# One scaled input for two norms, norm weights and shifts as columns at evictions, and a strict mask added by a matrix product, in the attention chain of a two-block network

## The reference

```python
def modulate(h, shift, scale):
    return h * (1.0 + scale[:, None, :]) + shift[:, None, :]
# keys and values: h = modulate(rmsnorm(x, kv_norm_g), shift, scale) @ kv_w, and k = rmsnorm(k per head, k_norm_g)
# queries:         h = modulate(rmsnorm(x, norm_mix_g[1]), sh1, sc1) @ w_q,  and q = rmsnorm(q per head, q_norm_g) * 64**-0.5
z = q . k                                        # 16 heads of 64, queries in blocks of 128
strict = jnp.arange(end)[None, :] < (t0 + jnp.arange(SB_BLOCK))[:, None]
log1m = jnp.where(strict, -jax.nn.softplus(z), 0.0)
between = lax.cumsum(log1m, axis=3, reverse=True) - log1m
a = jnp.where(strict, jnp.exp(jax.nn.log_sigmoid(z) + between), 0.0)
out = a @ v, then @ w_out
```

## Time and profile before

| what | value |
|---|---|
| median of 3 runs | 3055.77 us (3055.34 to 3058.81) |
| the profiled execution | 3056.06 us, span 3054.3 us |
| busy in the span | PE 67%, DVE 58%, ACT 28%, POOL 33% |
| mean granted clock of TensorE | 0.826 |
| POOL's gathers (L743) | 512 of u rows, 512 of v rows |
| DMA over the span | 862.77 MB, mean 282 GB/s |

### The profile page before, as it was taken

The page is one execution under the profiler, slowest core; times in us unless marked ns, Lnnn a source line. Parts: engine busy times, 40 slices in busy tenths (PEclk is TensorE's granted clock), DMA queues, the critical chain, the costliest instruction groups (busy, mean ns, idle before and its releaser), DMA issues.

```text
span 3054.3 us, 33874 instructions
## 1 busy us (share of the span) xinstructions
PE 2043.3 (67%) x11630; PEld 1413.7 (46%) x11630; DVE 1778.2 (58%) x3285; ACT 840.6 (28%) x1268; POOL 1011.0 (33%) x1063
## 2 busy tenths in 40 slices
PE   7888710355426746257520357998899989988998
PEld 3636400011112212122100014996799879877997
DVE  2365689913694356970769403666566566655664
ACT  3434200000021101221000002445554454555444
POOL 1000067777565575654777772001000000000000
PEclk9999955677757978569755677999899999999999
DMA  7575699999999999989999996554155545542553
GB/s 277 190 261 195 224 376 420 406 392 416 420 393 358 418 407 416 385 313 419 400 419 420 410 419 236 185 184 149 48 174 184 176 144 185 172 134 80 181 184 126
DMA packets 238775, 862.77 MB, mean 282 GB/s; under 512 B 27958, under 2 KB 28428, under 8 KB 238404
## 3 DMA queue, kind: packets, MB, share of 16 engines
q0 software_dynamic: 147456, 536.94, 43.9%
q1 hardware_dynamic: 87840, 318.81, 30.6%
q10 hardware_dynamic: 3364, 5.61, 0.6%
HBM read 860.18 MB, written 1.05 MB: 282 GB/s over the span
## 4 chain that ended last, share of the span: by engine, by line
PE 37%; DVE 16%; DMA 12%; issue 11%; POOL 10%; ACT 2%; DVEq 1%; ACTq 0%; POOLq 0%
PE ps L1417 17%; POOL sb_arena L743 10%; DVE sb_arena L2447 9%; DMA sb_arena<-in_peer_v,sb_arena 8%; PE ps L1428 7%; DMA sb_arena<-in_peer_u,sb_arena 4%; PE ps L831 4%; PE ps L1178 3%; PE ps L993 1%; DVE sb_w_lo L638 1%; PE ps L1211 1%; PE ps L1335 1%; PE ps L868 1%; ACT sb_arena L2000 0%; PE ps L1026 0%
## 5 line engine op out<-in xcount | busy, mean ns | idle before, releaser
L638 DVE TENSOR_TENSOR sb_w_lo<-sb_w,sb_w_hi 128x1024 fp32r<-128x1024 f32 (+2 forms) x393 | 470.6, 1212 | 330.9 <-ACT sb_w_hi L624 327.7
L2447 DVE CUSTOM_DVE_ANT_0 sb_arena<-sb_arena,ps 128x1024 f32<-128x1024 f32 x512 | 607.1, 1219 | 60.7 <-DMA sb_arena<-in_peer_u,sb_arena 50.4
L743 POOL DMA_INDIRECT sb_arena<-in_peer_u,sb_arena x512 | 486.2, 950 | 352.9 <-issue 118.8
L743 POOL DMA_INDIRECT sb_arena<-in_peer_v,sb_arena x512 | 494.8, 966 | 250.9 <-issue 140.7
L1178 PE MATMUL ps<-sb_arena 128*32 128x512 f32 x2048 | 349.9, 816 | 268.6 <-DMA sb_arena<-in_peer_v,sb_arena 265.9
L624 ACT ACTIVATE sb_w_hi<-sb_w 128x1024 fp32r<-128x1024 f32 (+2 forms) x398 | 407.5, 1040 | 291.7 <-DMA sb_w<-in_ffn 197.9
L1417 PE MATMUL ps<-sb_xT_hi,sb_w_hi 128*128 128x256 f32 x1408 | 400.2, 284 | 2.8 <-DVE sb_w_lo L638 2.8
L1417 PE MATMUL ps<-sb_xT_hi,sb_w_lo 128*128 128x256 f32 x1408 | 400.1, 284 | 0.0
L1417 PE MATMUL ps<-sb_xT_lo,sb_w_hi 128*128 128x256 f32 x1408 | 400.0, 284 | 0.0
L1178 PEld LDWEIGHTS ps<-sb_arena 128*32 128x32 f32 x2048 | 75.2, 131 | 524.6 <-issue 521.7
L638 POOL TENSOR_TENSOR sb_w_lo<-sb_w,sb_w_hi 128x1024 fp32r<-128x1024 f32 x5 | 11.7, 2350 | 918.9 <-ACT sb_w_hi L624 596.7
(11 more groups left out here) (426 smaller groups left out, 3001.7 us busy)
## 6 DMA issues: line engine op xcount, KB each, us to landing
sb_w<-in_ffn SPq DMA_DIRECT2D x264, 512.0 KB, 3.5
sb_w<-in_ada_w SPq DMA_DIRECT2D x112, 512.0 KB, 6.2
sb_w<-in_peer_w_q SPq DMA_DIRECT2D x48, 512.0 KB, 8.0
sb_w<-in_kv_w SPq DMA_DIRECT2D x32, 512.0 KB, 8.4
sb_w<-in_fox_w_in SPq DMA_DIRECT2D x24, 512.0 KB, 3.3
sb_w<-in_ma_w_vo SPq DMA_DIRECT2D x16, 512.0 KB, 3.5
sb_arena<-in_peer_u,sb_arena POOLq DMA_INDIRECT x512, 6.8
sb_arena<-in_peer_v,sb_arena POOLq DMA_INDIRECT x512, 6.7
```

The costliest lines, as they stand in the source:

```text
L638: e.tensor_tensor(lo, w, hi.bitcast(F32), ALU.subtract).then_inc(lo_ready, 1)
L743: pool.indirect_dma_start(ROW[:, r % ROWS, :], None, d[("peer_v" if kind else "peer_u") + str(layer)], bass.IndirectOffsetOnAxis(ap=(LISTE ...
L2447: v.tensor_tensor_reduce(out=x, in0=x, in1=PS[:, 0:2, :].rearrange("p a b -> p (a b)"), scale=1.0, scalar=0.0, op0=ALU.mult, op1=ALU.add, ...
```

## The change

- VectorE scales `x` by the root alone, once (`row_factor` and one `ts`), and TensorE transposes that once. ScalarE's evictions of the transposes, now eight of 128x128 for keys and eight for queries instead of two of 128x512 each, multiply with a column (norm weight times 1 + scale) and add a column (shift), which lie in `gain_cols`. The queries' transposed input has a buffer of its own (`w_xqT`) and a semaphore `queries_taken`.
- The weights of the head norms are multiplied in at the evictions of the transposed heads.
- `before` is gone. TensorE begins the diagonal block of each score bank with a product of `upto` and a new matrix `never` (zero but for -1e30 on the diagonal), which adds -1e30 wherever the key is not strictly earlier; the scores are accumulated on it. Both masks and the minimum with 0 go, and exp signals `att_ready` itself.
- Six small loads are added to ScalarE's in table 0 (20 instead of 14), 32 transposes of 1x128 on TensorE in its tick 4, and ScalarE's copies and 16 products of 128x1 that make the columns.
- Of the copies on all partitions only one (`norm_ffn_g1`) is left, loaded ahead of the stage and multiplied with 1 + scale once.
- The transpose of the list of experts is written in tick 8 of the u tables instead of tick 20.

```diff
+            pool.affine_select(out=never[:, :], in_=never[:, :], compare_op=ALU.not_equal, fill=-MASKED,
+                               base=0, pattern=[[-1, P]], channel_multiplier=1)
...
# PE
+                        for n, x in enumerate((mod(1), KVMOD[:, D:2 * D], mod(0), KVMOD[:, 0:D])):
+                            for k_ in range(KD):
+                                tr(PS[:, 3, 128 + KD * n + k_:129 + KD * n + k_], x[0:1, k_ * P:(k_ + 1) * P], ident[0:1, 0:1])
...
-                        if k == 20:
+                        if k == 8:
...
+                        for odd in range(2):
+                            mm(PS[:, 3 + odd, 0:(t + 1) * 2 * P].rearrange("p (a b s) -> p a b s", a=2, s=P)[:, :, t, :],
+                               upto[:, :], never[:, :].unsqueeze(1).to_broadcast([P, 2, P]), start=True, stop=False,
+                               skip_group_check=True)
...
-                    pe.wait_ge(SEM["normed"], 3 * t + 2)
-                    turned(H[:, t, :])
+                    pe.wait_ge(SEM["queries_taken"], t + 1)
...
# ACT
+                    def moved_in(dst, which, b, turn_):
+
+                        for c in range(4):
+                            scale, shift = moved(4 * b + c)[which]
+                            ins = f(dst[:, 4 * b + c, :], PS[:, 3 + turn_ % 2, c * P:(c + 1) * P], ACT.Identity,
+                                    scale=scale, bias=shift)
+                        return ins
...
-                    taken(w_kT[:, :, t * P:(t + 1) * P])
-                    next_gain(4, 4)
+                    taken(w_kT[:, :, t * P:(t + 1) * P], gain=gain_cols[:, KEY_GAIN:KEY_GAIN + 1])
...
-                        f(x, x, ACT.Exp).then_inc(SEM["exp_out"], 1)
+                        f(x, x, ACT.Exp).then_inc(SEM["att_ready"], 1)
...
# DVE
-                        dve.drain()
-                        masked(w_lost).then_inc(SEM["lost_ready"], 1)
+                        dve.drain().then_inc(SEM["lost_ready"], 1)
...
-                    norm(0, KVMOD[:, 0:D], KVMOD[:, D:2 * D])
+                    row_factor(1)
+                    ts(h, x, rs[:, ROOT:ROOT + 1], None, ALU.mult).then_inc(SEM["normed"], 1)
                     yield "norm for keys"
-                    dve.wait_ge(SEM["tile_turned"], 16 * t + 2)
-                    norm(1, mod(0), mod(1))
...
-                    for n, y in enumerate(both):
-                        tt(y, y, gain_of(2 + n, SD).unsqueeze(1).to_broadcast([P, SH, SD]), ALU.mult
...
-                           ALU.subtract)
-                        dve.drain()
-
-                        ts(y, y, 0.0, None, ALU.min).then_inc(SEM["exponent_in"], 1)
+                           ALU.subtract).then_inc(SEM["exponent_in"], 1)
                         yield "between"
-                        dve.wait_ge(SEM["exp_out"], 4 * t + g + 1)
-                        masked(y).then_inc(SEM["att_ready"], 1)
```

More of the change, by code:

```diff
@@ L86, in build @@
         after = sb("after", [P, P])
-        before = sb("before", [P, P])
+        never = sb("never", [P, P])
         upto = sb("upto", [P, P])
@@ L225, in build @@
         stage("weave", loads=loads * NT, gain=len(gains))
-        for _ in range(NT):
-            gains.extend([("kv_norm_g", D), ("norm_mix_g1", D), ("k_norm_g", SD), ("sb_q_norm_g", SD), ("norm_ffn_g1", D)])
+        gains.append(("norm_ffn_g1", D))
         def embed(i):
@@ L534, in build, with moved @@
         w_head_gains = WHF[:, 4224:4288]
+        WOVEN_GAINS = (("norm_mix_g1", KD), ("kv_norm_g", KD))
+        KEY_GAIN, QUERY_GAIN = 74, 75
+        def moved(n):
+            return [gain_cols[:, x + n:x + n + 1] for x in (84, 100)], [gain_cols[:, x + n:x + n + 1] for x in (76, 92)]
         def by_block(x, t):
@@ L691, in _ @@
             pool.memset(ones[:, :], 1.0)
+            pool.memset(never[:, :], 0.0)
             pool.memset(causal[:, :], 0.0)
@@ L1184, in chain @@
                 def chain(t):
-                    turns, cols, units = 16 * t, 12 * t, st["unit0"] + len(st["loads"]) // NT * t
+                    turns, cols, units = 14 * t, 12 * t, st["unit0"] + len(st["loads"]) // NT * t
                     def turned(src, jobs=2):
@@ L1199, in turned, with column @@
                             turns += 1
-                    def column():
+                    def column(x=w_xT):
                         nonlocal cols, units
@@ L1228, in scores @@
                                              w_kT[rows, g * HG // 2 + pair, b * P:(b + 1) * P],
-                                             w_qT[rows, g * HG // 2 + pair, :], start=True, stop=True)
+                                             w_qT[rows, g * HG // 2 + pair, :], start=b < t, stop=True,
+                                             skip_group_check=True)
                         pe.drain().then_inc(SEM["z_ready"], 1)
@@ L1723, in gather @@
                             row += n
+                        for name in ("k_norm_g", "sb_q_norm_g"):
+                            for c in range(2):
+                                act.dma_start(w_gains[row:row + 1, c * SD:(c + 1) * SD], d[name].unsqueeze(0)
+                                              ).then_inc(gains_loaded, 16)
+                            row += 1
+                        for name, n in WOVEN_GAINS:
+                            act.dma_start(w_gains[row:row + n, :], d[name].rearrange("(k p) -> k p", p=P)
+                                          ).then_inc(gains_loaded, 16)
+                            row += n
                         for row, name in enumerate(("fox_g_qn", "fox_g_kn", "mla_g_qn", "mla_g_kn")):
@@ L1794, in chain @@
                     stats(0)
-                    next_gain(1, 0)
                     yield "norm for keys"
-                    taken(w_xT)
-                    next_gain(2, 1)
+                    for b in range(2):
+                        act.wait_ge(SEM["tile_turned"], turns + b + 1)
+                        moved_in(w_xT, 0, b, turns + b).then_inc(SEM["tile_taken"], 1)
+                    for b in range(2):
+                        ins = moved_in(w_xqT, 1, b, turns + b)
+                    ins.then_inc(SEM["queries_taken"], 1)
+                    turns += 2
                     yield "turn for keys"
```

85 lines of the change are left out of this document (39 added, 46 removed).

## The result

The changed kernel takes 3049.23 us (median of 10 runs, 3044.88 to 3052.07) against 3057.05 us (3051.96 to 3060.36) for the kernel before on the same chip: ratio 0.9975, 95% interval 0.9965 to 0.9984. The gain is 8 us; 31 were predicted, and the time lies above the range. The profiled execution took 3050.52 us, span 3048.8.

A forecast was written before the change was run, and what follows sets the result against it. The gather stage was taken as bound by DMA at 420 GB/s, with VectorE later behind tick 13; 18.9 (VectorE) + 8.4 (change of table) + 3.75 (bytes) = 31 us off 3056.06 gave 3025 us, range 3010 to 3043.

The forecast's parts named there:

- the sum: Forecast gain: 18.9 us of VectorE's work, 8.4 at the change of table, 3.75 of bytes, together 31 us.
- VectorE behind tick 13: After the head sums: products, masks and minima removed from VectorE, 8.9 us in block 0, 10.0 in block 1.
- Rival B: Behind tick 13 irregularly landing rows swallow half of VectorE's 18.9 us: 3034 us; chance 0.18 (3030 to 3045).
- The change of table: Between VectorE's last dot and the GELU: shorter wait, 4.3 us in block 0, 4.1 in block 1, together 8.4.
- Bytes: In the gather stage: five 512 KB weight copies leave, three of them counted at 1.25 us each, 3.75 us.
- (a) the mask products: Ahead of each group's scores: two added TensorE products, 1 us per group, at most 2.1, hidden by 2.5 us slack.
- (b) the wait for `between`: Between a group's first `lost` and its `between`: VectorE may wait some 0.2 us where the mask went.
- (c) the sixteen evictions: Per block, 128x128 evictions replacing four of 128x512: at most 6 us of ScalarE, costing nothing; uncovered, 3 us per block.
- (d) the small loads: Table 0: six more loads on ScalarE's queue, first dot 1.6 to 2.1 us later, hidden; if not, +2 us.
- The word on POOL: Beside one-input VectorE operations gathers wait 0.26 us: eight minima removed save up to 2.1 us, new scalings cost 2 x 0.26.
- Rival A: In the gather stage all 41.7 us of losses and 6.25 us of bytes return: 3008 us; chance 0.12 (below 3015).
- Rivals C and D: C: scores-to-softplus path becomes the bound, 3065 us, chance 0.04; D: chain no shorter, only bytes go, 3052 us, 0.04.

The follow-up runs named there:

- the first experiment: The changed kernel with eight small tensors packed into one, so the gathers' slots start on a multiple of 256 bytes again: 3027.26 us, ratio 0.9900.
- the second: The kernel before with 128 unused bytes ahead of the arena, so the slots start 128 bytes past a multiple of 256: 3080.36 us, ratio 1.0076.

## Why the prediction was wrong

**The step that failed** is the first: "The rest of the stage is DMA-bound, and there only bytes count", at 420 GB/s and 1.25 us for a gather. The plateau was taken as a constant, and the losses and the sum were counted from it. It is not one: the same diff moved the slots 128 bytes, and a gather of 512 KB costs 1.28 us. For the stage's 1024 gathers that is 537 MB x (1/409.5 - 1/420) = 33 us at most, 8.2 for a pair of tables; the first experiment gives 22 and the second 23. Between the changed kernel and the first experiment tables 0 and 1 differ by all of it, 8.4 us, the pairs with the chain by only 4.3 and 5.3: from the head sums to the last dot VectorE takes the same 96 and 103 us in both kernels, whatever a gather costs. No part of the sum, of its bounds or of the rivals held a change of the DMA's own pace, and so the range was too narrow. With the slots on the boundary the time is 3027.3 us against 3025 forecast. The three kernels that differ from the changed one in memory layout alone and have the slots there gain 30 (packed tensors), 34 (all of memory) and 37 us (only the slots moved) over before; the sum's 31 fits them.

The diff line that did it was read, as more columns for weights and shifts. What was not done was to ask which tensor is allocated behind it.

**The prediction's other steps:**

- *VectorE behind tick 13, 18.9 us*: right in its mechanism, and in size as far as the runs tell. From head sums to the last dot it takes 95.8 us in block 0 (842.5 to 938.3), as forecast, and in block 1 1235.05 to 1338.5 = 103.5, 1.5 above. Put back, the work costs 17 us, with an uncertainty of about 7. Rival B (half swallowed, 9.5) is not supported: in neither block does VectorE wait for a row behind tick 13 in the changed kernel. All of its waits in block 1's stretch are these:

```profile
DVE sb_w_hi_whole L2577 <- PE ps L1255: 0.8, 1, 0.8
DVE sb_arena L2478 <- issue: 0.6, 4, 0.2
DVE sb_w_hi_whole L2567 <- issue: 0.4, 1, 0.4
```

- *The change of table, 8.4 us*: right in its mechanism (waits of 0.42 and 2.33 us where 0.5 and 2.4 were said); put back, it costs 12.5 us by the ratio with an uncertainty of about 7, 10 by the table pairs, and 8.7 in the two stretches that it lengthens.
- *Bytes, 3.75 us*: neither shown nor excluded.
- *(a) the mask products*: they took the upper bound in block 1, 2.08 us for the first group, and used the slack up: VectorE takes that group's first operation at 1258.89, 0.03 us after ScalarE's end (1257.80 + 1.06); it was 2.5 before. The cost is still nothing, but the cover is gone in that group.
- *(b) the wait for `between`*: one of 0.8 us, where some 0.2 was said.
- *(c) the sixteen evictions*: 5.7 us of ScalarE in block 0, within the 6 allowed.
- *(d) the small loads*: the first dot stands at 404.58 with 7.93 us of wait in place of 401.25 and 6.09. The 1.84 us more are those forecast. With the same loads tables 0 and 1 take 338.3 us from the first gather in the first experiment, 338.6 before: hidden, as said.
- *The word on POOL*, left out of the sum: in block 1 all four minima have a longer gather beside them, three of 1.20 us and one of 1.15. But so have masks, which work on two inputs: the gathers at 1281.96, 1305.96, 1308.99 and 1329.76 took 1.34, 1.15, 1.15 and 1.15 us, each issued 0.1 to 0.4 us into a mask. No run separates what this is worth.
- *Rival A* (3008 us): not reached; block 1 still waits 2.33 us for its GELU and POOL 6.61 for slots.
- *Rivals C and D*: out, by the doubled mask products and by the first experiment.
- *"Table 3 some 14 us earlier, table 5 some 31"*: on the boundary the chain's table pairs are 14.6 and 17.9 us shorter than before, 32.5 together; in the changed kernel, off it, only 10.4 and 12.7. "Near 420 in block 0" holds on the boundary (419) and not off it (409).

The list of what would make the prediction wrong named waits above 1 us in the chain, waits for rows, a late GELU and changes behind the stage; the first three did not come, and behind the stage nothing is told apart from the spread of 6 us. What did show the failure was the row that was to stay as it was, table 0 at 420 GB/s.

## What to carry to other kernels

When a kernel is bound by a stream of indirect gathers into SBUF, as this one is, the byte at which the buffers that they write start is part of the kernel: work it out before and after any change of an allocation ahead of it, and pin the buffers to multiples of 256 bytes. For the plain weight loads no gain was seen here. Read a stretch that the change doesn't touch first; if its rate moved, look at the layout. To judge a change by itself, hold the layout; here a gain of 1% was three quarters hidden by 128 bytes.

## What the runs showed of the hardware

Indirect gathers of rows of 4 KB ran at 420 GB/s into slots on multiples of 256 bytes in SBUF (607 x 256 in the kernel before, 608 x 256 where only the slots were moved) and at 409 to 410 into slots 32, 64, 128 or 192 bytes past one (128 in the kernel before too). The Trainium skill ("DMA: Bandwidth & Descriptors", section "How a descriptor splits into AXI transactions") says that a descriptor not starting on a multiple of 256 bytes has its first transaction started at the boundary below, with the bytes before it fetched unused. The traces agree that a start off this boundary costs, with 2.5%. An estimate from the page's count of beats: 32, 64, 128 and 192 bytes would cost 1, 2, 4 and 6 beats more than the 128 of a row, 0.8, 1.6, 3.1 and 4.7%. The runs show the same 2.5% for all of them, so the size is not that of the page, and the page speaks of reads where here the written side moved. Why every offset costs the same stays open.
